# Opening of a two-layer block: twelve of the modulation weights' tile loads go from SyncE's DMA queue to GpSimd's

## The reference, cut to what matters

```python
cond = jax.nn.silu(c)                       # 1 x 2048
mod = (cond @ mod_w[i] + mod_b[i])[:, None, :]   # mod_w: 2048 x 12288
sh1, sc1, ga1, sh2, sc2, ga2 = jnp.split(mod, 6, axis=-1)
h = x * (1 + sc1) + sh1
y = gated_deltanet(h, gdn_w_in[j], ...)     # first: proj = h @ w_in
```

## Time and profile before

| | |
|---|---|
| median of 3 runs | 2733.85 us (2733.78 to 2734.37) |
| the profiled execution's own time | 2733.77 us |
| its span, first to last instruction | 2732.2 us |
| mean granted TensorE clock | 0.995 |
| PE busy | 2682.0 us, 98% of the span |
| bytes of the first 32 mods | 32 loads of 1 MiB, all on SP's queue |

### The profile page before, as it was taken

One profiled execution on the slowest core, in us unless ns is written; L12 is line 12 of the kernel. 1 busy time (PEld: TensorE's weight loads), 2 busy tenths in 40 slices (PEclk: granted clock), 3 DMA queues, 4 the chain that ended last, 5 costly groups with the idle time before them and its releaser, 6 DMA issues.

```text
span 2732.2 us, 45343 instructions
## 1 busy us (share of the span) xinstructions
PE 2682.0 (98%) x17387; PEld 2248.0 (82%) x17387; DVE 1923.4 (70%) x2199; ACT 1211.7 (44%) x1572; POOL 879.6 (32%) x645
## 2 busy tenths in 40 slices
PE   6999999999999999999999999999999999999998
PEld 4798998899897888888888888889777778888887
DVE  1476787787788687666666666698999996655554
ACT  2355456545545445333333333354333334444344
POOL 1076676666666416300000000004656560000000
PEclk9999999999999999999999999999999999999999
DMA  9966666675666676666666666555555556666664
GB/s 364 355 217 202 231 227 203 227 239 191 222 229 195 204 224 225 186 189 189 190 185 189 189 190 185 185 162 163 172 162 173 171 165 184 183 189 187 189 203 154
DMA packets 283975, 552.53 MB, mean 202 GB/s; under 512 B 16881, under 2 KB 54322, under 8 KB 282674
## 3 DMA queue, kind: packets, MB, share of 16 engines
q1 hardware_dynamic: 263488, 473.49, 56.4%
q0 software_dynamic: 19472, 76.06, 7.3%
q10 hardware_dynamic: 866, 0.80, 0.1%
HBM read 548.19 MB, written 2.10 MB: 201 GB/s over the span
## 4 chain that ended last, share of the span: by engine, by line
PE 90%; DVE 6%; DMA 2%; ACT 1%; issue 1%; SPq 1%; DVEq 0%; ACTq 0%
PE pg L1203 37%; PE pd L1203 17%; PE pg L919 13%; PE pg L906 5%; PE pg L1190 3%; PE pd L832 2%; PE pg L938 2%; DVE wl L2292 2%; DMA arena<-in_mod_w 1%; PE pd L1061 1%; PE pd L1079 1%; DMA wr<-in_gdn_w_in 1%; PE pd L1366 1%; PE pd L1379 1%; PE pd L845 1%
## 5 line engine op out<-in xcount | busy, mean ns | idle before, releaser
L2292 DVE TENSOR_TENSOR wl<-wr,wh 128x1024 fp32r<-128x1024 f32 x616 | 781.1, 1278 | 450.5 <-ACT wh L1768 448.1
L1768 ACT ACTIVATE wh<-wr 128x1024 fp32r<-128x1024 f32 x616 | 652.7, 1061 | 949.8 <-PE pg L1203 601.1
L654 POOL TENSOR_TENSOR wl<-wr,wh 128x1024 fp32r<-128x1024 f32 x195 | 479.4, 2461 | 367.9 <-ACT wh L1549 233.2
L1203 PE MATMUL pg<-wh,hh 128*128 128x512 f32 x1344 | 532.6, 396 | 2.9 <-DVE wl L2292 1.5
L1203 PE MATMUL pg<-wl,hh 128*128 128x512 f32 x1344 | 526.9, 392 | 0.0
L1203 PE MATMUL pg<-wh,hl 128*128 128x512 f32 x1344 | 525.9, 391 | 0.0
L1549 ACT ACTIVATE wh<-wr 128x1024 fp32r<-128x1024 f32 x216 | 227.6, 1057 | 358.7 <-PE pg L919 196.6
L1203 PEld LDWEIGHTS pg<-wh,hh 128*128 128x128 f32 x1344 | 252.5, 188 | 71.0 <-issue 12.5
L919 PE MATMUL pg<-hh,wh 128*128 128x256 f32 x1024 | 300.1, 293 | 0.8 <-ACT arena L1609 0.8
L1203 PEld LDWEIGHTS pg<-wh,hl 128*128 128x128 f32 x1344 | 252.4, 188 | 56.4
L1203 PEld LDWEIGHTS pg<-wl,hh 128*128 128x128 f32 x1344 | 252.4, 188 | 53.0
(11 more groups left out here) (427 smaller groups left out, 4757.8 us busy)
## 6 DMA issues: line engine op xcount, KB each, us to landing
wr<-in_w_in SPq DMA_DIRECT2D x224, 512.0 KB, 4.1
wr<-in_ffn_w_gu SPq DMA_DIRECT2D x176, 512.0 KB, 3.8
wr<-in_gdn_w_in SPq DMA_DIRECT2D x128, 512.0 KB, 4.1
arena<-in_mod_w POOLq DMA_DIRECT2D x60, 1024.0 KB, 6.6
wr<-in_ffn_w_down SPq DMA_DIRECT2D x88, 512.0 KB, 4.6
arena<-in_mod_w SPq DMA_DIRECT2D x32, 1024.0 KB, 13.7
wr<-in_gdn_w_in SPq DMA_DIRECT2D x128, 256.0 KB, 3.0
wr<-in_gdn_w_out SPq DMA_DIRECT2D x56, 512.0 KB, 4.4
```

What stands on the lines that cost most here:

```text
L654: nc.gpsimd.tensor_tensor(wl[c % RING][:], wraw[c % 4], wh[c % RING][:].bitcast(F32), ALU.subtract)\
L1203: m = nc.tensor.matmul(halves(bank)[:, h, :], act[x][:, k0 + k, h * P:(h + 1) * P], w[s][:, k, :], skip_group_check=True, start=(first and ...
L1768: a(wh[c % 4][:], wraw[c % 4], ACT.Copy).then_inc(s_hc, 1)
L2292: v.tensor_tensor(wl[c % 4][:], wraw[c % 4], wh[c % 4][:].bitcast(F32), ALU.subtract).then_inc(s_lc, 1)
```

## The change: what it does

From mod 9 on, the odd mods (9, 11, ..., 31; twelve of them) are no longer issued by SP. POOL issues them in a loop behind its mask building, each with the wait that SP had for it (s_md >= t - 5), into the same buffers, and with three new semaphores (s_modp) that tell PE of their landing. Even mods, x and all chunks stay on SP, in the same order among themselves. PE's order of work is the same; only the semaphore that it waits for differs.

```diff
@@ semaphores
+        s_modp = [sem(f"s_modp{i}") for i in range(3)]
@@ SyncE: the loads of LOADS
                     if kind == "chunk":
                         gdn_load(0, n)
-                    else:
+                    elif n % 2 == 0:
                         mod_load(n)
@@ GpSimd: after the masks, before the low parts of chunks 21 to 23
+            for t in range(9, 32, 2):
+                pool.wait_ge(s_md, t - 5)
+                k, ch = 4 * (t % 4), MOD_SEQ[t // 4]
+                pool.dma_start(wm[t % 6], mod_w[:, k:k + 4, ch * 512:(ch + 1) * 512]).then_inc(s_modp[t % 6 // 2], 16)
             gcT = gx[:, 3, :]
             pool.wait_ge(s_low, 4 + 21)
@@ TensorE: mod_part
-                pe.wait_ge(s_mod[t % 6], 16 * (t // 6 + 1))
+                if t % 2 and t >= 9:
+                    pe.wait_ge(s_modp[t % 6 // 2], 16 * ((t - 9) // 6 + 1))
+                else:
+                    pe.wait_ge(s_mod[t % 6], 16 * (t // 6 + 1))
```

## The result

The changed kernel took 2738.28 us (median; 2737.54 to 2741.83), the kernel before, on the same chip, 2734.17 us: 4.1 us more, a ratio of 1.0014 with a 95% interval of 1.0007 to 1.002. That is inside the range on record and inside the 0.2% that were called no change, and on the slower side of the forecast of 2736.0; it is 0.2 us above the forecast's own range, which ended at 2738.1. The profiled execution's span is 2736.6 us against 2732.2, so its trace has 4.4 us to account for.

What follows compares the result with a forecast made beforehand. PE, busy 98% of the span, was taken to bound the kernel outside the opening, where the DMA engines are full. 5.2 - 3.0 + 0 = +2.2 us on 2733.77 gave 2735.97, as median 2736.0; own range 2734.3 to 2738.1, on record 2733.0 to 2740.0.

Steps and rivals of the forecast that it cites:

- SP's queue and POOL's issues cost nothing: In the opening: SP issuing twelve fewer loads and idle POOL issuing them, 0.80 us each, 9.6 in all, changes time by 0.
- Two loads ahead of chunk 0, +5.2: Before quarter 0: mods 9 and 11 pass SP's backlog at 2.6 us each, moving quarter 0's start from 43.3 to 48.5.
- Mod 7 then lands at 40.4: In the opening: mod 7, landing at 35.23 before, is delayed by both POOL loads; its chain too gives quarter 0 at 48.5.
- The third load, 0: Before quarter 0: mod 13, released between 39 and 41.5 us, could add 0 to 2.6 us; taken as 0.
- The two later waits, -3.0: Ahead of quarters 1 and 2: PE's waits of 1.37 and 1.63 us, behind chunks 6 and 12, go.
- The clock, 0: At quarter 0's start: TensorE's slow clock again lasts 3.8 us into it, costing 0; bounds about -1.5 and +1.9 us.
- From there on PE is full and the loads are ahead of it.: After the waits of quarters 1 and 2: PE runs without further waits, and odd mods are late nowhere; no added time.
- the rival called slower: At chunks 6 and 12: more POOL loads pass them, so both waits stay; 2739.0, or 2741.6 with a third load; chance 0.12.
- The sum 2.2: Whole program: predicted net change, 5.2 - 3.0 + 0 = +2.2 us on the profiled execution's 2733.77.
- the first rival: In the opening: POOL's loads come too late or slowly to pass chunk 0, nothing changes, 2733.8 us; chance 0.10.

## Why the prediction came out as it did, point by point

- *SP's queue and POOL's issues cost nothing.* Right as far as the trace shows: the engines stay full at the same GB/s, POOL has 34 us to spare.
- *Two loads ahead of chunk 0, +5.2.* Right: 5.08 in the changed kernel, 4.9 with these two loads alone, 3.2 with one, 4.9 with the same order on SP alone. That POOL's loads land after 6.1 us was wrong (9.0 to 13.0): the load of the earlier trace rows ran where the engines had room (a share of 0.88 from 156 to 163 us). SP's backlog in front of chunk 0 is longer still, so the sum stood. But two steps on the way were wrong.
- *"Mod 7 then lands at 40.4", and both chains give 48.5.* It landed at 37.8; mod 11 came too late to pass it. By the 9.0 us from landing to quarter 0 of the run with mod 9 alone, I estimate that mod 7's chain would have allowed quarter 0 at 46.8. The sum was saved by chunk 0, which both loads did pass.
- *The third load, 0.* Right, but not for the reason given. It was released at 40.1, as forecast, and its packets were to begin from about 41, when chunk 0 would still need the engines for 3.5 us. They began at about 44.5, since each POOL load took some 4 us from issue to first packet, which the prediction had at about 1.
- *The two later waits, -3.0.* Right: both gone, in every run in which quarter 0 started 3 us or more later.
- *The clock, 0.* Right here (3.9 us against 3.8); between runs the slow stretch after quarter 0's start varied from 2.8 to 4.7 us.
- *"From there on PE is full and the loads are ahead of it."* This step failed. Mod 29 passes chunk 13, mods 29 and 31 pass chunk 15, PE waits 0.49 and 1.28 us behind these chunks, and putting the two loads back removed both waits. It is the mechanism of the rival called slower, which I had priced at chunks 6 and 12, where it did not come (the waits there went), and not at the last chunks of quarter 2.
- The sum 2.2 thus became 2.2 - 0.1 + 1.8 = 3.9 in the opening. The remaining 0.5 us of the profiled execution arises between 1791 and 1848 us, where the clock fell at different moments of the two executions; its cause stays open.
- *The rule of the Trainium skill* (DMA: Bandwidth & Descriptors, "Issuing engines are not separate DMA queues") that one pool of engines serves all issuers agrees with the trace, at 383 GB/s before and after. Read as "so nothing changes", the first rival, it would have missed all of the 4.1 us, which come from who is served first.

## What to carry to other kernels

Where the DMA engines are full, a second queue brings no bytes sooner; it is a change of priority, and what it carries can go ahead of the first queue's backlog. Here it did so from about 4 us after the issue on, so what was to land sooner than that was not passed. Look at what it passes: the price is the time of the bytes that go ahead, 2.3 to 2.7 us for each MiB here, paid where PE waits for what was passed. Look at when it is released, too: a PE that is late releases the buffers later. Where the waits of quarters 1 and 2 were removed by themselves, another of more than 1 us took their place.

## What I had not expected of the hardware

- Loads issued by POOL took 9.0 to 13.0 us to land beside SP's full queue (median 9.7), against 6.1 us at 156 us into the program before. About 4 us of that passed before the first packet. They still passed loads of SP: SP's last eight mods took 7.2 to 20.1 us (median 14.5).
- With both queues at work the engines served them packet for packet (191 and 190 packets from 24 to 27 us), so POOL's, with packets twice as large, had two thirds of the bytes.
- The clock can fall behind short waits of PE, which then costs more than the waits: after waits of 1.8 and 1.8 us the granted clock was 0.50 for 3.4 us in one run, after one of 1.72 us for 3.4 us in another, while with 0.7 and 1.2 us in the same place it stayed at full. It does not always: in the first of these runs it stayed at full after a wait of 2.05 us ahead of quarter 1.
